# A two-layer hybrid decoder step: page numbers clamped once and read without range checks, and the prompt's compression joined to the paged rounds

## The reference, cut to what matters

```
old_mla = cache_mla[li, page_table]                  # sample attention of layer 0
old     = cache_nsa_kv[li, page_table, :, 0:2]       # keys and values to be compressed
kp, vp  = cache_nsa_kv[li, page, rows, 2:4]          # the selected branch

def nsa_compress(k, pe, phi1, phi2):                 # blocks of 64 positions
    kb = k.reshape(B, nc, 64, G, d) + pe             # the position table is added
    return silu(kb.reshape(.., 64 * d) @ phi1) @ phi2
```

## Time and profile before

| what | value |
|---|---|
| three runs | 3036.63, 3043.06, 3044.13 us; median 3043.06 |
| profiled execution | 3044.95 us, span 3043.1 us, 67474 instructions |
| TensorE busy | 2627.5 us, 86% of the span |
| VectorE, ScalarE, GpSimd busy | 1188.7, 828.3, 124.1 us |
| HBM | 289.86 MB read, 30.27 MB written, 105 GB/s over the span |
| page reads | 512 of 144 KB (MLA samples, 16 of them early), 512 of 128 KB (compression), 512 of 128 KB (NSA samples) |

### The profile page before, as it was taken

The page is one execution under the profiler, slowest core; times in us unless marked ns, Lnnn a source line. Parts: engine busy times, 40 slices in busy tenths (PEclk is TensorE's granted clock), DMA queues, the critical chain, the costliest instruction groups (busy, mean ns, idle before and its releaser), DMA issues. The chain is left out here.

```text
span 3043.1 us, 67474 instructions
## 1 busy us (share of the span) xinstructions
PE 2627.5 (86%) x24822; PEld 1722.3 (57%) x24822; DVE 1188.7 (39%) x3103; ACT 828.3 (27%) x1926; POOL 124.1 (4%) x217
## 2 busy tenths in 40 slices
PE   6999888899995559799998799978888887888878
PEld 4556455566664444345546688856666665555534
DVE  2121345545544932101100000036666665666633
ACT  1111344433332210001100000025556554444400
POOL 0000000011110100000000000000000001222100
PEclk9999899999998679899998899999999998989989
DMA  4000200177775141331106477630000003777732
GB/s 177 23 15 13 68 1 1 33 219 223 223 216 97 21 149 56 118 144 49 39 27 179 146 226 224 198 131 2 2 2 2 2 2 113 220 213 225 237 112 75
DMA packets 313027, 321.33 MB, mean 106 GB/s; under 512 B 72587, under 2 KB 289979, under 8 KB 312380
## 3 DMA queue, kind: packets, MB, share of 16 engines
q1 hardware_dynamic: 226268, 233.55, 24.9%
q10 hardware_dynamic: 86432, 83.47, 9.1%
HBM read 289.86 MB, written 30.27 MB: 105 GB/s over the span
## 5 line engine op out<-in xcount | busy, mean ns | idle before, releaser
L2203 PE MATMUL bank<-cm_room 64*64 64x114 f32 (+1 forms) x4608 | 296.9, 441 | 5.9 <-DMA cm_room<-cache_nsa_kv 5.7
L2203 PEld LDWEIGHTS bank<-cm_room 64*64 64x64 f32 x4608 | 253.0, 163 | 46.8 <-DMA cm_room<-cache_nsa_kv 6.8
L2023 PE MATMUL bank<-cm_room 128*128 128x512 f32 (+3 forms) x576 | 225.0, 551 | 0.0
L2507 PE MATMUL bank<-ident,np_p 128*128 128x128 f32 x1056 | 160.7, 282 | 41.0 <-ACT np_pT L2597 21.5
L2589 ACT ACTIVATE np_p<-np_p,np_nmax 128x640 f32<-128x640 f32 (+7 forms) x256 | 184.6, 726 | 8.1 <-DVE np_nmax L2644 8.1
L314 PE MATMUL bank<-ev_hT,ev_w 128*128 128x384 f32 (+1 forms) x576 | 177.9, 469 | 6.1 <-ACT zaT L257 6.1
L2498 PE MATMUL bank<-kk,np_q 64*128 64x320 f32 (+5 forms) x832 | 151.6, 474 | 31.9 <-DVE np_nmax L2644 24.8
L2023 PEld LDWEIGHTS bank<-cm_room 128*128 128x128 f32 (+1 forms) x576 | 103.9, 182 | 117.3 <-issue 106.4
L2522 PEld LDWEIGHTS bank<-kv,np_pT 128*64 128x64 f32 x4224 | 133.4, 138 | 53.2 <-issue 49.1
L954 PE MATMUL bank<-ident,ms_pg 128*128 128x128 f32 x1024 | 133.4, 283 | 31.5 <-DMA ms_pg<-cache_mla 23.4
L2597 ACT ACTIVATE np_pT<-bank 128x512 f32<-128x512 f32 (+1 forms) x208 | 109.2, 531 | 175.8 <-PE bank L2507 175.5
(11 more groups left out here) (519 smaller groups left out, 3844.9 us busy)
## 6 DMA issues: line engine op xcount, KB each, us to landing
ms_pg<-cache_mla SPq DMA_DIRECT2D x388, 144.0 KB, 2.7
ns_pg<-cache_nsa_kv SPq DMA_DIRECT2D x320, 128.0 KB, 2.8
cm_room<-cache_nsa_kv ACTq DMA_DIRECT2D x262, 128.0 KB, 4.0
cm_room<-cache_nsa_kv SPq DMA_DIRECT2D x250, 128.0 KB, 4.1
ns_pg<-cache_nsa_kv ACTq DMA_DIRECT2D x192, 128.0 KB, 3.3
ms_pg<-cache_mla ACTq DMA_DIRECT2D x124, 144.0 KB, 3.5
ev_w<-w_in_even SPq DMA_DIRECT2D x8, 768.0 KB, 11.2
cm_room<-w_in_odd SPq DMA_DIRECT2D x24, 256.0 KB, 6.7
```

Of the source, the lines that this page charges most:

```text
L2023: t = nc.tensor.matmul(bank[:n, f, 0:hi - lo], hT[:, i // 3 % 2, k, at:at + n], wt[:, k, lo:hi], start=k == 0, stop=k == KD - 1)
L2203: t = nc.tensor.matmul(out(blk)[kind * HD:(kind + 1) * HD], phi[blk * BLK:(blk + 1) * BLK, kind, x, :], rows(kind, blk, x), start=x == 0, ...
L2507: t = nc.tensor.transpose(bank[:, f, (m - lo) * P:(m - lo + 1) * P], p[:, u % NB, hd, b * P:(b + 1) * P], c["ident"][:])
```

## The change

The table is clamped once, on the chip, and every place that loads page numbers leaves the range checks out (the same argument on all four lines). The compression has PRE = 9 more pages at the front: page 0 is the position table, copied four times per half of the partitions from memory, pages 1 to 8 are the prompt's tiles, copied by VectorE. CU is 58, so 521 pages still make 9 rounds. Column 0 of round 0 is the bias, columns 2 to 17 are the prompt's hidden values; the products of lines 2238 and of `own_rows` are gone, and the prompt's second products come after round 1. The sample rows `tk` and the hidden tiles move into memory that is free by then.

```diff
+CLAMPED = "load_constants clamps every page number to the pool on the chip"
...
+        @block.vector
+        def _(dve):
+            dve.wait_ge(s_load, 48)
+            nc.vector.tensor_scalar(c["pages"][:], c["pages"][:], 0.0, float(POOL - 1), ALU.max, ALU.min)
...
-            _, pages = nc.values_load_multi_w_load_instructions(c["pages"][0:1, first:first + count], engines=[kind], min_val=0, max_val=POOL - 1)
+            _, pages = nc.values_load_multi_w_load_instructions(c["pages"][0:1, first:first + count], engines=[kind], min_val=0, max_val=POOL - 1, skip_runtime_bounds_check_because=CLAMPED)
...
-        early["soon"], early["mid"] = soon, (soon + CU + 1) // 2
-        tk = sb("op_tk", [NS, 6 * KVW])
+        early["soon"], early["mid"] = PRE + soon, (PRE + soon + CU + 1) // 2
+        tk = place(6 * KVW)[:NS]
...
-                phi_pages(nc, act, mybir.EngineType.Activation, a, c, early, 0, 0, soon)
+                phi_pages(nc, act, mybir.EngineType.Activation, a, c, early, 0, PRE, PRE + soon)
...
-CU = 57
-CP = DB * NPAGE
+PRE = 1 + NTILE
+CU = 58
+CP = PRE + DB * NPAGE
...
-    eng.dma_start(early["pe"][:, half, :], a[("nsa_pe_k", "nsa_pe_v")[half]][0]).then_inc(early["s_w"], 16)
+    for kind, pe in enumerate(("nsa_pe_k", "nsa_pe_v")):
+        for gg in range(NG):
+            eng.dma_start(pg[rows, 0, 0, (NG * kind + gg) * HD:(NG * kind + gg + 1) * HD], a[pe][0]).then_inc(early["s_w"], 16)
...
-        hid = sb("cm_hid", [P, 2, 2, 2 * NPAGE])
-        hidp = sb("cm_hidp", [P, 2, NC])
+        hid = kv[:, 0:2, 0:2 * KVW].rearrange("p b (h n) -> p b h n", h=2)
+        hidp = kv[:, 2, 0:2 * NC].rearrange("p (h n) -> p h n", h=2)
...
-                act.wait_ge(S["bias"], 1)
-                nc.scalar.activation(bias[:], bank[:, 4, 0:1], ACT.Copy).then_inc(S["biasd"], 1)
-
-                act.wait_ge(S["accp"], 1)
+                act.wait_ge(S["acc"], 1)
+                nc.scalar.activation(bias[:], bank[:, 0, 0:1], ACT.Copy).then_inc(S["biasd"], 1)
                 act.wait_ge(S["biasd"], 1)
-                nc.scalar.activation(hidp[:], bank[:, 0:2, 0:NC], ACT.Silu, bias=bias[:]).then_inc(S["hidp"], 1)
+                act.wait_ge(S["own"], 1)
+                nc.scalar.activation(hidp[:], bank[:, 0:2, 2:2 + NC], ACT.Silu, bias=bias[:]).then_inc(S["hidp"], 1)
...
-                pe.wait_ge(s_w, 16 * 8)
-                for x in range(HD):
-                    for kind in range(2):
-                        t = nc.tensor.matmul(bank[kind * HD:(kind + 1) * HD, 4, 0:1], phi[:BLK, kind, x, :], pe_sb[:, kind, x:x + 1], start=x == 0, stop=x == HD - 1)
-                t.then_inc(S["bias"], 1)
...
-                hidden(lambda blk: bank[:, blk, 0:NC].rearrange("p (i g) -> p i g", g=NG), own_rows).then_inc(S["accp"], 1)
-                pe.wait_ge(S["hidp"], 1)
...
+                pe.wait_ge(s_w, 16 * 14)
+                pe.wait_ge(S["own"], 1)
+
+                def own_products():
+                    pe.wait_ge(S["hidp"], 1)
...
+                    if n == 1:
+                        own_products()
...
+                nc.vector.tensor_copy(pg[:, 0, 1:PRE, :], kv[:, :, 0:2 * KVW]).then_inc(S["own"], 1)
```

More of the change, by code:

```diff
@@ L556, in _ @@
                 for first, at in ((0, 0), (4, 4), (8, 8), (3 * NPAGE // 4, 12)):
-                    _, pages = nc.values_load_multi_w_load_instructions(c["pages"][0:1, first:first + 4], engines=[mybir.EngineType.SP], min_val=0, max_val=POOL - 1)
+                    _, pages = nc.values_load_multi_w_load_instructions(c["pages"][0:1, first:first + 4], engines=[mybir.EngineType.SP], min_val=0, max_val=POOL - 1, skip_runtime_bounds_check_because=CLAMPED)
                     for j, page in enumerate(pages, at):
@@ L1870, in odd_projection @@
         soon = 20
-        assert at >= PHI_EL + soon * 2 * KVW
+        assert at >= PHI_EL + (PRE + soon) * 2 * KVW
         wq = place(KD * NW).rearrange("p (k n) -> p k n", k=KD)
@@ L2142, in phi_load @@
 def phi_load(eng, a, early, half):
-    phi = phi_room(early)[0]
+    phi, pg = phi_room(early)
     rows = slice(half * BLK, (half + 1) * BLK)
@@ L2155, in phi_pages @@
         last = min(first + 16, hi)
-        _, pages = nc.values_load_multi_w_load_instructions(c["pages"][0:1, n * CU + first:n * CU + last], engines=[kind], min_val=0, max_val=POOL - 1)
+        _, pages = nc.values_load_multi_w_load_instructions(c["pages"][0:1, n * CU + first - PRE:n * CU + last - PRE], engines=[kind], min_val=0, max_val=POOL - 1, skip_runtime_bounds_check_because=CLAMPED)
         for j, page in enumerate(pages, first):
@@ L2173, in compress @@
         phi, pg = phi_room(early)
-        phi2, pe_sb, s_w, s_page = (early[k] for k in ("phi2", "pe", "s_w", "s_page"))
+        phi2, s_w, s_page = (early[k] for k in ("phi2", "s_w", "s_page"))
         bias = sb("cm_bias", [P, 1])
-        hid = sb("cm_hid", [P, 2, 2, 2 * NPAGE])
-        hidp = sb("cm_hidp", [P, 2, NC])
-        names = ["bias", "acc", "hid", "out", "ev", "dv", "accp", "biasd", "hidp", "outp", "evp"]
+        hid = kv[:, 0:2, 0:2 * KVW].rearrange("p b (h n) -> p b h n", h=2)
+        hidp = kv[:, 2, 0:2 * NC].rearrange("p (h n) -> p h n", h=2)
+        names = ["own", "acc", "hid", "out", "ev", "dv", "biasd", "hidp", "outp", "evp"]
         S = {n: cleared(nc, ctx, "cm_s_" + n) for n in names}
         SP, AC = mybir.EngineType.SP, mybir.EngineType.Activation
+        fetched = [size - (PRE if n == 0 else 0) for n, size in enumerate(sizes)]
         segments = []
         for n, size in enumerate(sizes):
-            at = n * CU
+            at = max(n * CU, PRE)
             while at < n * CU + size:
-                b = at // NPAGE
-                to = min((b + 1) * NPAGE, n * CU + size)
-                segments.append((n, b, at - n * CU, at - b * NPAGE, to - at))
+                b = (at - PRE) // NPAGE
+                to = min(PRE + (b + 1) * NPAGE, n * CU + size)
+                segments.append((n, b, at - n * CU, at - PRE - b * NPAGE, to - at))
                 at = to
@@ L2234, in _ @@
             def _(pe):
[L2235 to L2250 removed]
+                pe.wait_ge(s_w, 16 * 14)
+                pe.wait_ge(S["own"], 1)
+                def own_products():
+                    pe.wait_ge(S["hidp"], 1)
+                    nc.tensor.matmul(bank[:HD, 5, 0:2 * NC], phi2[:HD], hidp[:HD].rearrange("p h n -> p (h n)"), start=True, stop=True)
+                    for gg in range(NG):
+                        t = nc.tensor.matmul(bank[:2 * NTILE, 6, gg * HD:(gg + 1) * HD], hidp[HD:].rearrange("p h (i g) -> p g (h i)", g=NG)[:, gg, :], phi2[HD:], start=True, stop=True)
+                    t.then_inc(S["outp"], 1)
                 def products(b):
@@ L2270, in _ @@
                 for n, size in enumerate(sizes):
-                    pe.wait_ge(s_page[n % 2], 16 * sum(sizes[n % 2:n + 1:2]))
+                    pe.wait_ge(s_page[n % 2], 16 * sum(fetched[n % 2:n + 1:2]))
                     if n >= 2:
@@ L2278, in _ @@
                     hidden(lambda blk: bank[:, 2 * (n % 2) + blk, 0:2 * size].rearrange("p (j g) -> p j g", g=NG), rows).then_inc(S["acc"], 1)
-                    while ready < DB and n >= 1 and (ready + 1) * NPAGE <= n * CU:
+                    if n == 1:
+                        own_products()
+                    while ready < DB and n >= 1 and PRE + (ready + 1) * NPAGE <= n * CU:
                         products(ready)
@@ L3581, in build @@
                              "phi2": wide.enter_context(nc.sbuf_tensor("cm_phi2", [P, HD], F32)),
-                             "pe": wide.enter_context(nc.sbuf_tensor("cm_pe", [BLK, 2, HD], F32)),
                              "s_w": cleared(nc, wide, "cm_s_w"),
```

4 lines of the change are left out of this document (removed).

## The result

2914.15 us median (2905.03 to 2915.42, 4 runs) against 3040.28 (3036.63 to 3044.13, 4 runs) for the kernel before: ratio 0.9579, interval 0.9554 to 0.9603. The profiled execution took 2913.6 us with a span of 2911.8, 131.3 us less than before.

The account below looks back on a forecast made before the run. The prediction took SP's issuing, not memory, to pace the MLA stage; compression 32, MLA 20 and NSA 38, less 0.7 for the clamp, gave 89 us: 3044.95 - 89 = 2956, 2954 by the median; range 2928 to 2996.

Parts of the forecast that it names:

- the rival built on that sentence: All stages: transfers, not SP, set the pace, so only the joined compression gains; 3024 us, 3022 by the median; chance 0.12.
- the two terms of the checks there: Compression: without checks, issuing starts 4.1 us earlier after the barrier, and 5.7 us of DMA waits between rounds go.
- 283 / 27 = 10.5 us per step: MLA stage before the change: step pace taken from the value products of the last 28 steps.
- The pace forecast for TensorE: MLA stage: with checks gone TensorE paces at 9.8 us per step, taken from a stretch of four steps.
- The bound that stood beside it: MLA stage: upper bound of the gain, 23.4 us of page waits plus clock losses, 31 us; 20 was taken.
- the waits in full, letting the clock pay for what is given back: NSA stage: gain taken as 38 us, all removable waits, with no separate sum for the clock.
- 37.5 us were to go: NSA stage: removable waits of 21.5 us for pages, 11.1 at score transposes and some 5 at key transposes.
- up to 25 us more: NSA stage: what TensorE's clock could give back if no pause lets it fall; used only in the upper bound of 70.
- half is given back: Rival: the NSA stage meets its next bound at once, 15 us there and 15 in MLA; 2984 us, chance 0.12.
- rings fill: Rival: queues issue faster than rings drain, and blocked ScalarE issues delay NSA key copies; 3200 us, chance 0.04.
- the 0.6 named as a sign: NSA stage: ScalarE's mean issue rising above 0.6 us would show the forecast wrong.
- The range ended at 48: NSA stage: gain behind the range's lower end of 2928 us, its waits and less than half of its clock.

Follow-up runs that it names:

- Experiment 10: Changed kernel, without checks, but SP loads its 12 page numbers five times per MLA step and uses all five loads; 2956.95 us, ratio 0.9703.
- own7: Changed kernel with SP reading seven and ScalarE one of an NSA unit's eight pages, instead of five and three; 2970.69 us, ratio 0.9751.
- Experiment 5: Changed kernel with the range checks back on the page numbers of the compression alone; 2923.87 us, ratio 0.9603.
- the 13 profiles: Profiles whose MLA stage is that of the changed kernel or of the old kernel with only clamp and check removal; that stage took 327.4 to 335.8 us.
- Experiment 11: Changed kernel with TensorE made to wait for GpSimd once in each of seven NSA sequences; 2951.02 us, ratio 0.9692.

## Why the prediction was wrong

The forecast for the profiled execution was 2956 us, and it took 2913.6. Of the 42 us between them 18.5 lie in the NSA stage, 14.8 in the MLA stage and 2.0 in the compression; 5.4 lie in the first projection, which is no part of the change, and the rest in other stages.

**Bound and mechanism: right.** The two sample stages were held by the issuing queues and not by the memory. Experiment 10 shows it for the MLA stage with no check in the program: 3 us more of SP's time per step bring back the whole loss. For the NSA stage own7 shows it, also without a check: with more reads and longer loads on SP, waits for pages come back and the stage takes 351.1 us. The Trainium skill's page "DMA: Bandwidth & Descriptors", section "Issuing engines are not separate DMA queues", calls sequencer time usually small beside the transfer. The forecast set the check against the issue, where the page speaks of the issue against the transfer. For a single read the trace agrees with the page: on SP it takes 0.33 us to issue and 2.9 us (median) from issue to landing in the changed kernel's MLA stage. But a queue's issues follow one another, one read every 0.52 us, while its reads overlap, and the rival built on that sentence, 3022 us, did not come.

**Compression: right.** Start 21.8 us after the projection where 21.2 were forecast, rounds without a wait for pages, 34.0 us where 32 were forecast. Experiment 5 confirms the two terms of the checks there, some 4 us at the start (3.4) and 5.7 between rounds (9.4).

**MLA samples: 34.8 where 20 were forecast.** The failed step is the pace of the kernel before, "283 / 27 = 10.5 us per step". That mean runs over the last three steps too, which take 6.6 us each; in the last two no more pages are turned. From the first set of products to the 29th the steps took 306.7 / 28 = 10.95 us. The pace forecast for TensorE, 9.8, was right: it is 274.9 / 28 = 9.82. (10.95 - 9.82) x 28 = 32 us; the start of the stage gained 5.7 us more, and the wait for the last page, which was not there before, gave 3.2 back. Its length is chance: against the 13 profiles the gain is 30 to 38 us. The bound that stood beside it, waits and clock summed to 31, was nearer than the value taken.

**NSA samples: 56.5 where 38 were forecast.** The failed step is "the waits in full, letting the clock pay for what is given back". It put the clock at nothing in the sum, and the clock is a term of its own, the larger part of the miss. Over the whole stage, before and after, TensorE's busy time for the same 3432 products fell by 24.0 us and its idle time by 32.6 us (63.5 to 30.9):

```profile
2548.86:2896.70 347.84, 284.38 (x3432) 173.07 (x3432) 214.14 (x540) 141.32 (x360) 65.29 (x64) 0.88 0.72 220
...
2472.00:2763.30 291.30, 260.42 (x3432) 162.98 (x3432) 213.26 (x540) 143.23 (x360) 65.11 (x64) 0.96 0.83 263
```

The waits were forecast too high, and this hid a part of it: 37.5 us were to go, and 30.7 did (21.5 and 11.1, less the 1.9 by which those at the key transposes rose, where 5 were to go). The text had the clock's gain, "up to 25 us more", as a bound and not in the sum. With 24.0 for it, 62 would have stood against 56.5.

Experiment 11 shows the cause as far as a run can: pauses alone, with queues and reads as in the changed kernel, bring 0.50 behind each of them and 13.1 us of busy time. The trace of the kernel before shows the same without an added pause: from 2580 to 2881 us it has twelve stretches at 0.50, of 3.41 or 6.83 us, and each begins during a wait for pages or for ScalarE of 1.5 to 3.9 us or at most 1.2 us behind one. In the changed kernel's seven sequences, where no wait is above 1.2 us, there is none. Two waits of the kernel before, and the stretch at 0.50 that begins in the second:

```profile
2670.41 0.63 PE L3002 MATMUL bank<-ident,ns_s 128*128 128x128 f32 x4 [1.63 <-ACT ns_kT L2904]
2674.98 1.97 PE L2985 MATMUL bank<-ident,ns_pg 128*128 128x128 f32 x8 [3.94 <-DMA ns_pg<-cache_nsa_kv]
...
2672.75:2679.58 6.83, 4.60 (x44) 2.67 (x44) 1.37 (x7) 1.79 (x4) 5.08 (x5) 0.50 0.69 220
```

**Clamp, moved tiles, "half is given back", "rings fill":** the clamp took 0.41 us, and the first load behind its barrier was issued 0.5 us later (4.43 instead of 3.91); 0.7 was forecast, with a part for a semaphore's hop for which no row stood. The longest ScalarE issue in the NSA stage was 2.07 us, but the median stayed at 340 ns and the mean at 0.40 us, below the 0.6 named as a sign: single issues took long, and the queue did not. Half was not given back in either stage. The range ended at 48 for the NSA stage, with less than half of the clock's term in it, and so missed 56.5.

What stays open: why the first projection takes 281 us in some profiles and 287 in others; it is no part of the change.

## What to carry to other kernels

Before calling a plateau of throughput the memory's limit, add up one step of the issuing queue: number loads, checks and issues here filled 10.0 of 10.95 us. Where a wait of TensorE goes and a stretch at a granted clock of 0.50 stood behind it, count two terms: the wait's own length, and what the stretch cost in busy time for the same products, here a little under half of the stretch (13.1 of 30.7 us in experiment 11, 21.5 of 49.5 in the seven sequences of the kernel before). Take a pace only over steps that do the same work, and don't add the costs of two queues that feed one step: either alone may hold it.

## What the runs showed of the hardware

- Behind six of the seven pauses of 3.45 us TensorE's granted clock was 0.50 for 3.41 us, behind the other for 6.83 us; one more such stretch of 3.41 us came 2 us after a wait of 1.78 us for ScalarE. In the kernel before, such stretches stand behind waits of about 2 us too, but not behind each: after waits of 2.07 us (NSA stage, to 2796.2) and 2.22 us (MLA stage, to 735.5) the clock stayed at 1.00.
- A load of page numbers on SP took 0.75 us for 12 numbers, but 0.95 and 2.1 to 2.4 us in turn for 10, and 1.17 and 2.9 to 3.2 in turn for 14. The slow ones begin at a number that is not a multiple of four (10, 30, ... and 14, 42, ...); ScalarE's, of 4, 8 or 12 numbers from multiples of four, took 0.31, 0.55 and 0.78 us. That it is the start of the read was not tried by itself.
- The 44 small loads of the state-space layer cost more spread over the MLA steps (289.6 instead of 274.9 us for 28 steps) than in one batch behind it, where one page read landed 10.2 us after its issue (888.0 to 898.2).
